# Centring the value rows in the transposing product, and a new order of the steps behind the mixing

## The chip, the cores and the metric

One core of one Trainium2 chip runs the program. The time is device microseconds of an execution; the figure for a kernel is the median of its runs.

## What is computed

The reference is one transformer block with two mixing branches over 16 meta and 512 data tokens, width 1024. Cut to what matters here:

```python
y = rwkv7_scan(rh, heads(decay), kh, vh, kk, ah)      # per head of 64: S += v k^T ..., y = S r
mu = jnp.mean(y, axis=-1, keepdims=True)
var = jnp.mean(jnp.square(y - mu), axis=-1, keepdims=True)
y = ((y - mu) * lax.rsqrt(var + GN_EPS)).reshape(B, T, RW_WIDTH)
y = y * ln_gain.astype(f32) + ln_bias.astype(f32)
bonus = jnp.sum(rh * kh * r_k, axis=-1, keepdims=True) * vh
y = (y + bonus.reshape(B, T, RW_WIDTH)) * g.astype(f32)
...
merged = (sigmoid(gate_sb) * (o_sb @ w_branch_sb) + sigmoid(gate_rw) * (o_rw @ w_branch_rw))
```

The state S is zero at the start, and each value row of it, so each y, is linear in the value vector v of its head: if the mean over a head's 64 values is taken off v, y has the mean zero. The bonus uses v with its mean.

## The kernel before

All activations stand transposed, channels on partitions and tokens along the row, four tiles of 128 channels ("pairs" p of two heads). Each matrix product is made of three: weights and activations are split into a high and a low part (w_hi, w_lo; h_hi, h_lo), and high x high, high x low, low x high are summed in PSUM (`products`, L531 to L541). Weights come in units of 128 x 1024: SyncE fetches a unit into one of four raw buffers, ScalarE writes its high part (`hi_unit`, L525), VectorE its low part (`lo_unit`, L530), into one of two pairs of buffers, which TensorE must have left.

The stages are: norm of the input; 26 units that make the projections; the mixing, in which nine chunks of 64 tokens of the recurrent branch run beside eight heads of attention and ten units of gates, in orders written out by hand for each engine (`ORDER_PE` and so on); the stage behind the mixing, which this change is about; eight branch units; the output product; the FFN.

In a chunk of the mixing, `T0`, `T1`, `T2` (L1488 to L1495) transpose b, k and v of the chunk: products of a 64 x 64 piece with an identity (`st_id`, columns K_IST of the constants tile), two heads apart in the two halves of the partitions. VectorE copies T2's result to v_tm, from where the state and the output take it. `bonus` is made earlier, from vv itself.

Behind the mixing, the order is the list `LATE`, from which each engine takes its own part in the order of the list. Its items are, for r = 0 and 1 (two pairs of heads each, q = 0 and 1): `mean` (TensorE multiplies y with the block matrix `blk`, L1592; VectorE subtracts, L1178; ScalarE squares, L882), `var` (TensorE, L1598; ScalarE square root, L888; VectorE reciprocal, L1182), `gate` (TensorE's gate product, L1604; VectorE y times reciprocal, L1187; ScalarE gain and bias, L894; GpSimd adds the bonus, L692), `out` (VectorE times the gate, L1194; ScalarE high part orw_hi, L899; GpSimd low part orw_lo, L695). `osb` is the split of the attention output (ScalarE osb_hi L876, GpSimd osb_lo L685). Between them stand units: 0 to 5 are gate units (24 products each; ScalarE applies the sigmoid, L915, then splits the weights of the unit two further on), unit 0's products having been made at the end of the mixing already; from 6 on they are branch units. Branch unit 6 multiplies the attention output first (12 products), then waits for all `post` steps of VectorE and GpSimd before the 12 with orw_hi and orw_lo. In the list each engine runs strictly in order:

```python
LATE = [("osb", 0), ("mean", 0), ("unit", 0), ("unit", 1), ("var", 0), ("mean", 1), ("unit", 2), ("gate", 0),
        ("out", 0), ("unit", 3), ("var", 1), ("unit", 4), ("gate", 1), ("out", 1), ("unit", 5)]
```

Of the kernel before, what the change touches and what calls it, by code (L numbers as in the profile page):

```python
# [41 lines left out]
HD = 64  # L42
# [23 lines left out]

K_ID, K_TRI, K_CTRI, K_BLK, K_LT, K_LE, K_IST, K_RST = 0, 128, 256, 384, 512, 576, 640, 704
NK = K_RST + T
# [10 lines left out]
for _p in range(PAIRS):  # L79
# [33 lines left out]

POST_ITEMS = {"mean": (["mean0", "mean1"], ["sq0", "sq1"], ["centre0", "centre1"], []),
              "var": (["var0", "var1"], ["root0", "root1"], ["recip0", "recip1"], []),
              "gate": (["gate0", "gate1"], ["gain0", "gain1"], ["norm0", "norm1"], ["bonus0", "bonus1"]),
              "out": ([], ["hi0", "hi1"], ["out0", "out1"], ["lo0", "lo1"])}

LATE = [("osb", 0), ("mean", 0), ("unit", 0), ("unit", 1), ("var", 0), ("mean", 1), ("unit", 2), ("gate", 0),
        ("out", 0), ("unit", 3), ("var", 1), ("unit", 4), ("gate", 1), ("out", 1), ("unit", 5)]  # L120
LATE += [("unit", i) for i in range(2 * AHEAD, len(MERGE) - EARLY)]
# [120 lines left out]
def build(nc, x, meta, w_in, w_sb, w_rw, w_out, w_g, w_u, w_d, decay_up, aaa_up, gate_up,  # L242
          vecs, g_mix_pre, g_mix_post, g_ffn_pre, g_ffn_post, kf, kb, out):
    with ExitStack() as ctx:
# [463 lines left out]
        def _(act):  # L708
# [161 lines left out]
            for kind, i in LATE:  # L870
                if kind == "osb":
# [4 lines left out]
                    s_.activation(osb_hi[:], qT[:], ACT.Copy).then_inc(osb_h, 1)  # L876
                if kind == "mean":
                    for q in range(2):
                        act.wait_ge(post_dve, upto(POST_DVE, "post", i, f"centre{q}"))
                        if i:  # L880
                            act.wait_ge(post_pe, upto(POST_PE, "post", i - 1, f"var{q}"))
                        s_.activation(ysq[q][:], y_of(2 * i + q), ACT.Square).then_inc(post_act, 1)  # L882
# [109 lines left out]
        def _(dve):  # L992
# [179 lines left out]

            for kind, i in LATE:
                if kind == "mean":
                    for q in range(2):
                        dve.wait_ge(post_pe, upto(POST_PE, "post", i, f"mean{q}"))
                        y = y_of(2 * i + q)
                        v_.scalar_tensor_tensor(y, bank(4 + q), -1.0 / HD, y, ALU.mult, ALU.add).then_inc(post_dve, 1)  # L1178
                if kind == "var":
# [126 lines left out]
        def _(pe):  # L1306
# [111 lines left out]
            def identity(k, p):  # L1418
                return st_id[k, :]

            def of_batch(t, e):
                return lambda k, p: t[k, p // 2, 2 * e + p % 2, :]
# [12 lines left out]
            for kind, n, s in ORDER_PE:  # L1435
# [44 lines left out]
                if kind == "seq":  # L1480
# [9 lines left out]
                    if s in ("T0", "T1", "T2"):  # L1490
                        pe.wait_ge(mix_dve, last_of(MIX_DVE, "seq", c, ("aak", "ark", "arb")))
                        if c != LAST_C:
                            pe.wait_ge(mix_pool, last_of(MIX_POOL, "seq", c, ("bh", "kh")))
                        t = (bt, kt, vv)[int(s[1])]
                        mm = heads(SB_, 128 * int(s[1]), C, 1, [(0, lambda k, p: t[k, p, cols(c)], identity)])  # L1495
                    if s == "Z1":
# [87 lines left out]
            for kind, i in LATE:  # L1584
                if kind == "osb":
                    pe.wait_ge(mix_act, len(MIX_ACT))
                    pe.wait_ge(mix_dve, len(MIX_DVE))
                if kind == "mean":
                    for q in range(2):
                        if i:  # L1590
                            pe.wait_ge(post_dve, upto(POST_DVE, "post", i - 1, f"centre{q}"))
                        t_.matmul(bank(4 + q), blk, y_of(2 * i + q), start=True, stop=True).then_inc(post_pe, 1)  # L1592
                if kind == "var":
# [5 lines left out]
                if kind == "gate":  # L1599
                    for q in range(2):  # L1600
                        if i:
                            pe.wait_ge(post_dve, upto(POST_DVE, "post", i, f"centre{q}"))
                        f0 = (2 * i + q) * P
# [96 lines left out]
def tables():  # L1700
# [11 lines left out]
    f[:, K_LE:K_LE + C] = s <= t  # L1712
    f[:, K_IST:K_IST + C] = s == t
    f[:, K_RST:K_RST + T] = (np.arange(T)[None, :] + PAD) % C != 0
    b = np.zeros((P, NB), np.float32)
# [31 lines left out]
```

## Time and profile before

| | |
|---|---|
| median of 3 runs | 971.79 us (969.87 to 972.54) |
| the profiled execution | 973.85 us |
| its span | 972.1 us, mean granted clock 0.976 |
| TensorE products / weight loads busy | 930.8 us (96%) / 744.4 us |
| VectorE / ScalarE / GpSimd busy | 477.8 / 401.4 / 74.0 us |
| the mixing | from 199 to 450.4 us of the span |
| behind it, to the branch products | 450.4 to 497.6 us |
| from there to the end | 474.5 us |

### The profile page before, as it was taken

To read this page: it belongs to the slowest core of one execution; us is meant where nothing else is said; L and a number is where in the kernel's file an instruction comes from. 1 tells how busy PE (TensorE), PEld (TensorE's weight loads), DVE (VectorE), ACT (ScalarE), POOL (GpSimd) and SP (SyncE) were. 2 spreads that over 40 slices of the span, in tenths; PEclk is the share of its full clock that TensorE was granted. 3 is DMA by queue.
4 is the path that set the end of the run, shared out by engine and by line. 5 is a ranking of instruction groups with operands and counts; after the bars stand their busy time and mean duration, and the time that the engine had idled before them with its cause. 6 is when DMAs were issued, how large, how long until landed. Compare 5 with 4: busy or idle time off the path is not lost.

```text
span 972.1 us, 18946 instructions
## 1 busy us (share of the span) xinstructions
PE 930.8 (96%) x8213; PEld 744.4 (77%) x8213; DVE 477.8 (49%) x618; ACT 401.4 (41%) x576; POOL 74.0 (8%) x99
## 2 busy tenths in 40 slices
PE   4999999989999999999989996999999999999997
PEld 3999999856667777766768785888888888888886
DVE  6357776236575356362657653444444444422243
ACT  5344455356665445454534452332223223221141
POOL 1011212111111011001220000000000000000000
PEclk9999999969899999999989997999999999999999
DMA  8322222301110101121216641223333233332321
GB/s 258 104 85 69 87 65 67 91 19 35 34 35 16 43 17 54 49 60 51 66 38 212 218 138 44 86 86 91 103 97 97 86 96 98 91 104 87 109 87 65
DMA packets 108863, 81.13 MB, mean 83 GB/s; under 512 B 2879, under 2 KB 99433, under 8 KB 108793
## 3 DMA queue, kind: packets, MB, share of 16 engines
q1 hardware_dynamic: 108792, 80.09, 27.2%
q8 instruction: 57, 0.93, 0.4%
q14 instruction: 14, 0.11, 0.0%
HBM read 75.36 MB, written 4.72 MB: 82 GB/s over the span
## 4 chain that ended last, share of the span: by engine, by line
PE 90%; DVE 4%; ACT 3%; issue 1%; POOL 1%; DMA 1%; SPq 0%; POOLq 0%; DVEq 0%; ACTq 0%
PE psum L540 47%; PE psum L1633 16%; PE psum L1395 9%; PE psum L1429 6%; PE psum L1543 3%; PE psum L1565 2%; PE psum L1580 2%; PE psum L1561 2%; DVE y_rec L1182 1%; PE psum L1316 1%; PE psum L1578 1%; ACT w_hi L525 1%; DMA x_in<-in_x 1%; PE psum L1365 0%; PE psum L1349 0%
## 5 line engine op out<-in xcount | busy, mean ns | idle before, releaser
L540 PE MATMUL psum<-h_hi,w_hi 128*128 128x512 f32 (+1 forms) x784 | 247.1, 352 | 3.3 <-DVE h_lo L999 1.7
L540 PE MATMUL psum<-h_lo,w_hi 128*128 128x512 f32 (+1 forms) x784 | 244.0, 348 | 0.0
L540 PE MATMUL psum<-h_hi,w_lo 128*128 128x512 f32 (+1 forms) x784 | 242.9, 346 | 0.0
L540 PEld LDWEIGHTS psum<-h_hi,w_hi 128*128 128x128 f32 x784 | 137.6, 190 | 25.7 <-issue 3.9
L540 PEld LDWEIGHTS psum<-h_lo,w_hi 128*128 128x128 f32 x784 | 136.8, 190 | 19.8 <-issue 1.2
L540 PEld LDWEIGHTS psum<-h_hi,w_lo 128*128 128x128 f32 x784 | 136.9, 190 | 18.7
L530 DVE TENSOR_TENSOR w_lo<-w_raw,w_hi 128x1024 fp32r<-128x1024 f32 x69 | 84.7, 1228 | 120.5 <-ACT w_hi L525 120.1
L1271 DVE TENSOR_TENSOR w_lo<-w_raw,w_hi 128x1024 fp32r<-128x1024 f32 x44 | 53.9, 1225 | 138.7 <-ACT w_hi L977 138.7
L525 ACT ACTIVATE w_hi<-w_raw 128x1024 fp32r<-128x1024 f32 x70 | 73.7, 1054 | 82.1 <-PE psum L1633 63.2
L977 ACT ACTIVATE w_hi<-w_raw 128x1024 fp32r<-128x1024 f32 x44 | 46.5, 1056 | 72.5 <-PE psum L540 72.5
L1633 PE MATMUL psum<-w_hi,act_hi 128*128 128x512 f32 x144 | 45.7, 389 | 0.0
L1633 PE MATMUL psum<-w_hi,act_lo 128*128 128x512 f32 x144 | 45.7, 389 | 0.0
L1633 PE MATMUL psum<-w_lo,act_hi 128*128 128x512 f32 x144 | 45.6, 389 | 0.0
L1543 PE MATMUL psum<-qT,kT 64*128 64x512 f32 (+4 forms) x80 | 35.4, 561 | 3.3 <-DVE tri_r L1092 3.2
L974 ACT ACT_TABLE_LOAD x11 | 14.1, 1283 | 54.8 <-PE psum L540 54.8
L1429 PE MATMUL psum<-h_hi,w_hi 128*128 128x512 f32 x80 | 34.8, 435 | 0.1
L974 ACT ACTIVATE ffn_t<-psum 128x512 f32<-128x512 f32 x22 | 13.2, 600 | 50.5 <-PE psum L540 50.4
L1170 DVE TENSOR_TENSOR scores<-scores,psum 128x128 f32<-128x128 f32 (+4 forms) x40 | 20.9, 523 | 26.5 <-PE psum L1565 26.3
L1113 DVE COPY_PREDICATED x_inv<-byte_masks,psum 128x512 f32<-128x512 uint8 (+1 forms) x25 | 16.9, 677 | 33.8 <-PE psum L1395 33.7
L1429 PE MATMUL psum<-h_lo,w_hi 128*128 128x512 f32 x80 | 32.3, 404 | 0.0
L1429 PE MATMUL psum<-h_hi,w_lo 128*128 128x512 f32 x80 | 32.1, 401 | 0.0
L1633 PEld LDWEIGHTS psum<-w_hi,act_hi 128*128 128x128 f32 x144 | 26.9, 188 | 5.8 <-DVE w_lo L530 0.2
(260 smaller groups left out, 1472.9 us busy)
## 6 DMA issues: line engine op xcount, KB each, us to landing
w_raw<-in_w_in SPq DMA_DIRECT2D x42, 512.0 KB, 3.8
w_raw<-in_w_g SPq DMA_DIRECT2D x22, 512.0 KB, 3.7
w_raw<-in_w_u SPq DMA_DIRECT2D x22, 512.0 KB, 3.7
w_raw<-in_w_d SPq DMA_DIRECT2D x22, 512.0 KB, 3.5
w_raw<-in_w_out SPq DMA_DIRECT2D x8, 512.0 KB, 5.4
kept_gates<-gate_raw SPq DMA_DIRECT2D x10, 256.0 KB, 2.3
sig_t<-kept_gates SPq DMA_DIRECT2D x10, 256.0 KB, 2.9
x_in<-in_x SPq DMA_DIRECT2D x4, 512.0 KB, 6.4
```

Source lines behind the costliest of these rows:

```text
L525: nc.scalar.activation(split(u)[0][:], raw[u % RAW][:], ACT.Copy).then_inc(w_hi_done, 1)
L530: nc.vector.tensor_sub(lo[:], raw[u % RAW][:], hi[:].bitcast(F32)).then_inc(w_split, 1)
L540: mm = nc.tensor.matmul(o, w[:, (w0 + i) * P:(w0 + i + 1) * P], xs[:, k, c0:c1], start=(n == 0), stop=(n == total - 1))
L974: s_.activation(ffn_t[t][:], bank(2 * t), ACT.Sigmoid).then_inc(f_sig, 1)
L977: s_.activation(w_hi[v % SPL][:], raw[v % RAW][:], ACT.Copy).then_inc(w_hi_done, 1)
L1170: v_.tensor_tensor(d, d, psum[0:rows, CBANK, SEQ - WIDTH[j]:SEQ], ALU.subtract).then_inc(mix_dve, 1)
L1271: v_.tensor_sub(w_lo[v % SPL][:], raw[v % RAW][:], w_hi[v % SPL][:].bitcast(F32)).then_inc(w_split, 1)
L1395: mm = t_.matmul(psum[rows(p, hd, moved), bnk + p // 2, o0:o0 + n], w(k, p), m(k, p), start=first, stop=last, skip_group_check=True)
L1429: mm = t_.matmul(bank(GBANK), w[:, k * P:(k + 1) * P], xs[:, k, META:T], start=(k == 0 and i == 0), stop=(k == KT - 1 and i == 2))
L1543: t_.matmul(psum[0:kn, QBANKS[j % 2], 0:WIDTH[j]], kT[lanes, hp, k0:k0 + kn], qT[lanes, hp, SEQ - WIDTH[j]:SEQ], start=True, stop=True).th ...
L1561: t_.matmul(psum[:, CBANK, SEQ - WIDTH[i]:SEQ], tri_r[:, P:2 * P], part[:, OFF[i]:OFF[i] + WIDTH[i]], start=False, stop=False, skip_group_ ...
L1633: mm = t_.matmul(bank(2 * b + h), xs[:, k, P * b:P * b + P], w[:, 512 * h:512 * h + 512], start=(k == 0 and i == 0), stop=(k == n - 1 and ...
```

## The change

It adds a matrix to the constants tile (identity minus 1/64, 64 columns, K_CEN) and uses it as T2's right operand in place of the identity. The four mean products and the four subtractions behind the mixing are left out, together with the waits on them, and the item `mean` becomes `square`. And `LATE` has another order: both `var` items stand earlier, against the units and against `out`.

```diff
--- before.py
+++ after.py
@@ -64,7 +64,7 @@
 NVEC = 42
 
 
-K_ID, K_TRI, K_CTRI, K_BLK, K_LT, K_LE, K_IST, K_RST = 0, 128, 256, 384, 512, 576, 640, 704
+K_ID, K_TRI, K_CTRI, K_BLK, K_LT, K_LE, K_IST, K_CEN, K_RST = 0, 128, 256, 384, 512, 576, 640, 704, 768
 NK = K_RST + T
 
 NB = LEVELS * C
@@ -111,13 +111,13 @@
 BATCHES = [tuple(range(c, min(c + 2, NC_))) for c in range(0, NC_, 2)]
 
 
-POST_ITEMS = {"mean": (["mean0", "mean1"], ["sq0", "sq1"], ["centre0", "centre1"], []),
+POST_ITEMS = {"square": ([], ["sq0", "sq1"], [], []),
               "var": (["var0", "var1"], ["root0", "root1"], ["recip0", "recip1"], []),
               "gate": (["gate0", "gate1"], ["gain0", "gain1"], ["norm0", "norm1"], ["bonus0", "bonus1"]),
               "out": ([], ["hi0", "hi1"], ["out0", "out1"], ["lo0", "lo1"])}
 
-LATE = [("osb", 0), ("mean", 0), ("unit", 0), ("unit", 1), ("var", 0), ("mean", 1), ("unit", 2), ("gate", 0),
-        ("out", 0), ("unit", 3), ("var", 1), ("unit", 4), ("gate", 1), ("out", 1), ("unit", 5)]
+LATE = [("osb", 0), ("square", 0), ("unit", 0), ("var", 0), ("square", 1), ("unit", 1), ("gate", 0), ("unit", 2),
+        ("var", 1), ("out", 0), ("unit", 3), ("gate", 1), ("unit", 4), ("out", 1), ("unit", 5)]
 LATE += [("unit", i) for i in range(2 * AHEAD, len(MERGE) - EARLY)]
 POST_PE, POST_ACT, POST_DVE, POST_POOL = (
     [("post", r, step) for item, r in LATE if item in POST_ITEMS for step in POST_ITEMS[item][e]] for e in range(4))
@@ -874,9 +874,8 @@
                     act.wait_ge(mix_pe, len(MIX_PE))
                     act.wait_ge(eps_ok, 2)
                     s_.activation(osb_hi[:], qT[:], ACT.Copy).then_inc(osb_h, 1)
-                if kind == "mean":
+                if kind == "square":
                     for q in range(2):
-                        act.wait_ge(post_dve, upto(POST_DVE, "post", i, f"centre{q}"))
                         if i:
                             act.wait_ge(post_pe, upto(POST_PE, "post", i - 1, f"var{q}"))
                         s_.activation(ysq[q][:], y_of(2 * i + q), ACT.Square).then_inc(post_act, 1)
@@ -1171,11 +1170,6 @@
                                          ALU.subtract).then_inc(mix_dve, 1)
 
             for kind, i in LATE:
-                if kind == "mean":
-                    for q in range(2):
-                        dve.wait_ge(post_pe, upto(POST_PE, "post", i, f"mean{q}"))
-                        y = y_of(2 * i + q)
-                        v_.scalar_tensor_tensor(y, bank(4 + q), -1.0 / HD, y, ALU.mult, ALU.add).then_inc(post_dve, 1)
                 if kind == "var":
                     for q in range(2):
                         dve.wait_ge(post_act, upto(POST_ACT, "post", i, f"root{q}"))
@@ -1417,6 +1411,9 @@
 
             def identity(k, p):
                 return st_id[k, :]
+
+            def centring(k, p):
+                return consts[k, K_CEN:K_CEN + C]
 
             def of_batch(t, e):
                 return lambda k, p: t[k, p // 2, 2 * e + p % 2, :]
@@ -1492,7 +1489,8 @@
                         if c != LAST_C:
                             pe.wait_ge(mix_pool, last_of(MIX_POOL, "seq", c, ("bh", "kh")))
                         t = (bt, kt, vv)[int(s[1])]
-                        mm = heads(SB_, 128 * int(s[1]), C, 1, [(0, lambda k, p: t[k, p, cols(c)], identity)])
+                        mm = heads(SB_, 128 * int(s[1]), C, 1,
+                                   [(0, lambda k, p: t[k, p, cols(c)], centring if s == "T2" else identity)])
                     if s == "Z1":
                         pe.wait_ge(mix_dve, upto(MIX_DVE, "seq", c, "v"))
                         mm = opening(SB_, 0, C, 0, (0, a_c, whole(s_st)))
@@ -1585,11 +1583,6 @@
                 if kind == "osb":
                     pe.wait_ge(mix_act, len(MIX_ACT))
                     pe.wait_ge(mix_dve, len(MIX_DVE))
-                if kind == "mean":
-                    for q in range(2):
-                        if i:
-                            pe.wait_ge(post_dve, upto(POST_DVE, "post", i - 1, f"centre{q}"))
-                        t_.matmul(bank(4 + q), blk, y_of(2 * i + q), start=True, stop=True).then_inc(post_pe, 1)
                 if kind == "var":
                     for q in range(2):
                         pe.wait_ge(post_act, upto(POST_ACT, "post", i, f"sq{q}"))
@@ -1598,8 +1591,6 @@
                         t_.matmul(bank(6 + q), blk, ysq[q][:], start=True, stop=True).then_inc(post_pe, 1)
                 if kind == "gate":
                     for q in range(2):
-                        if i:
-                            pe.wait_ge(post_dve, upto(POST_DVE, "post", i, f"centre{q}"))
                         f0 = (2 * i + q) * P
                         t_.matmul(bank(2 + 2 * i + q), gup[:, f0:f0 + P], sg[:, META:T], start=True, stop=True).then_inc(post_pe, 1)
                 if kind == "unit":
@@ -1711,6 +1702,7 @@
     f[:, K_LT:K_LT + C] = s < t
     f[:, K_LE:K_LE + C] = s <= t
     f[:, K_IST:K_IST + C] = s == t
+    f[:, K_CEN:K_CEN + C] = (s == t) - 1.0 / HD
     f[:, K_RST:K_RST + T] = (np.arange(T)[None, :] + PAD) % C != 0
     b = np.zeros((P, NB), np.float32)
     for j in range(LEVELS):
```

What stands on TensorE behind the last chunk, before (a_r holds y, consts is blk; of the 24 products of a unit only the first is shown, unit 1 first):

```order
L1592 MATMUL psum<-a_r,consts 128x512 [waits mix_dve,mix_act]
L1592 MATMUL psum<-a_r,consts 128x512
L540 MATMUL psum<-h_hi,w_hi_55 128x512 [waits w_split]
...
L1598 MATMUL psum<-y_sq_157,consts 128x512 [waits post_act]
L1598 MATMUL psum<-y_sq_158,consts 128x512 [waits post_act]
L1592 MATMUL psum<-a_r,consts 128x512 [waits post_dve] x2
L540 MATMUL psum<-h_hi,w_hi_53 128x512 [waits gate_out,w_split]
...
L1604 MATMUL psum<-sig_xg,gate_up_w 128x512 x2
L540 MATMUL psum<-h_hi,w_hi_55 128x512 [waits gate_out,w_split]
...
L1598 MATMUL psum<-y_sq_157,consts 128x512 [waits post_act]
L1598 MATMUL psum<-y_sq_158,consts 128x512 [waits post_act]
```

and in the changed kernel (L1591 is the variance product, L1595 the gate's):

```order
L1591 MATMUL psum<-y_sq_157,consts 128x512 [waits post_act,mix_dve,mix_act]
L1591 MATMUL psum<-y_sq_158,consts 128x512 [waits post_act]
L540 MATMUL psum<-h_hi,w_hi_55 128x512 [waits w_split]
...
L1595 MATMUL psum<-sig_xg,gate_up_w 128x512 x2
L540 MATMUL psum<-h_hi,w_hi_53 128x512 [waits gate_out,w_split]
...
L1591 MATMUL psum<-y_sq_157,consts 128x512 [waits post_act]
L1591 MATMUL psum<-y_sq_158,consts 128x512 [waits post_act]
L540 MATMUL psum<-h_hi,w_hi_55 128x512 [waits gate_out,w_split]
```

The variance product of the first two pairs now stands directly behind the mixing and waits for the squares; the second one stands behind unit 2 where it stood behind unit 3.

ScalarE before: from unit 1's sigmoid (sig_t_146) to the first root (y_rs), and from pair 0's high parts to the second pair's roots (L525 is the high part of a unit's weights):

```order
L915 ACTIVATE sig_t_146<-psum 128x512 [waits w_used]
L525 ACTIVATE w_hi_55<-w_raw_52 128x1024 [waits w_used,w_landed3]
L888 ACT_TABLE_LOAD
L888 ACTIVATE y_rs_161<-psum,small 128x512 [waits post_pe]
...
L899 ACTIVATE orw_hi<-y_o_163 128x512 [waits post_dve]
L899 ACTIVATE orw_hi<-y_o_164 128x512 [waits post_dve]
L915 ACTIVATE sig_t_148<-psum 128x512 [waits w_used]
L525 ACTIVATE w_hi_55<-w_raw_50 128x1024 [waits w_used,w_landed1]
L888 ACT_TABLE_LOAD [waits post_dve]
L888 ACTIVATE y_rs_161<-psum,small 128x512 [waits post_pe]
L888 ACTIVATE y_rs_162<-psum,small 128x512 [waits post_dve,post_pe]
```

and in the changed kernel:

```order
L887 ACT_TABLE_LOAD
L887 ACTIVATE y_rs_161<-psum,small 128x512 [waits post_pe]
L887 ACTIVATE y_rs_162<-psum,small 128x512 [waits post_pe]
...
L914 ACT_TABLE_LOAD
L914 ACTIVATE sig_t_146<-psum 128x512 [waits w_used]
...
L887 ACT_TABLE_LOAD [waits post_dve]
L887 ACTIVATE y_rs_161<-psum,small 128x512 [waits post_pe]
L887 ACTIVATE y_rs_162<-psum,small 128x512 [waits post_dve,post_pe]
L898 ACTIVATE orw_hi<-y_o_163 128x512 [waits post_dve]
L898 ACTIVATE orw_hi<-y_o_164 128x512 [waits post_dve]
L914 ACT_TABLE_LOAD
L914 ACTIVATE sig_t_148<-psum 128x512 [waits w_used]
```

The first roots stand ahead of unit 1's sigmoid and weights, the second ones ahead of pair 0's high parts and of unit 3's sigmoid.

VectorE before, from the first reciprocal to the low part of unit 6's weights:

```order
L1182 RECIPROCAL y_rec_159<-y_rs_161 128x512 [waits post_act]
L1182 RECIPROCAL y_rec_160<-y_rs_162 128x512 [waits post_act]
L1178 SCALAR_TENSOR_TENSOR a_r<-psum,a_r 128x512 [waits post_pe] x2
L530 TENSOR_TENSOR w_lo_54<-w_raw_49,w_hi_53 128x1024 [waits w_hi_done]
L1187 TENSOR_TENSOR a_r<-a_r,y_rec_159 128x512 [waits post_dve]
L1187 TENSOR_TENSOR a_r<-a_r,y_rec_160 128x512 [waits post_dve]
L1194 TENSOR_TENSOR y_o_163<-psum,a_r 128x512 [waits post_pe,post_pool]
L1194 TENSOR_TENSOR y_o_164<-psum,a_r 128x512 [waits post_pe,post_pool]
L530 TENSOR_TENSOR w_lo_56<-w_raw_50,w_hi_55 128x1024 [waits w_hi_done]
L1182 RECIPROCAL y_rec_159<-y_rs_161 128x512 [waits post_act]
L1182 RECIPROCAL y_rec_160<-y_rs_162 128x512 [waits post_act]
L530 TENSOR_TENSOR w_lo_54<-w_raw_51,w_hi_53 128x1024 [waits w_hi_done]
```

and in the changed kernel, from the low part of unit 2's weights to that of unit 5's:

```order
L530 TENSOR_TENSOR w_lo_54<-w_raw_51,w_hi_53 128x1024 [waits w_hi_done]
L1176 RECIPROCAL y_rec_159<-y_rs_161 128x512 [waits post_act]
L1176 RECIPROCAL y_rec_160<-y_rs_162 128x512 [waits post_act]
L530 TENSOR_TENSOR w_lo_56<-w_raw_52,w_hi_55 128x1024 [waits w_hi_done]
L1181 TENSOR_TENSOR a_r<-a_r,y_rec_159 128x512 [waits post_dve]
L1181 TENSOR_TENSOR a_r<-a_r,y_rec_160 128x512 [waits post_dve]
L530 TENSOR_TENSOR w_lo_54<-w_raw_49,w_hi_53 128x1024 [waits w_hi_done]
L1176 RECIPROCAL y_rec_159<-y_rs_161 128x512 [waits post_act]
L1176 RECIPROCAL y_rec_160<-y_rs_162 128x512 [waits post_act]
L1188 TENSOR_TENSOR y_o_163<-psum,a_r 128x512 [waits post_pe,post_pool]
L1188 TENSOR_TENSOR y_o_164<-psum,a_r 128x512 [waits post_pe,post_pool]
L530 TENSOR_TENSOR w_lo_56<-w_raw_50,w_hi_55 128x1024 [waits w_hi_done]
```

The second pair of reciprocals now stands ahead of pair 0's outputs (y_o) and of the low part of unit 5's weights.

## Rows read from the trace of the kernel before

**Rows 1.** The page's part 4: shares of the chain that ended last
```profile
PE 90%; DVE 4%; ACT 3%; issue 1%; POOL 1%; DMA 1%; SPq 0%; POOLq 0%; DVEq 0%; ACTq 0%
```

**Rows 2.** Chain of waits, 436 to 500: start us, us, what
```profile
461.56 6.56 DVE y_rec L1182 x2
...
482.99 6.56 DVE y_rec L1182 x2
```

**Rows 3.** Timeline of PE, 450 to 502: start, duration, line, names, shapes, count [idle before]
```profile
450.40 1.99 PE L1592 MATMUL psum<-a_r,consts 128*128 128x512 f32 x4 [0.48 <-ACT a_r L832]
...
457.79 1.88 PE L1598 MATMUL psum<-y_sq,consts 128*128 128x512 f32 x4
...
461.45 0.39 PE L540 MATMUL psum<-h_lo,w_hi 128*128 128x512 f32 x1
...
466.77 1.88 PE L1604 MATMUL psum<-sig_xg,gate_up_w 128*128 128x512 f32 x4
...
490.69 0.50 PE L540 MATMUL psum<-osb_hi,w_hi 128*128 128x512 f32 x1 [1.86 <-DVE w_lo L530]
...
497.56 0.47 PE L540 MATMUL psum<-orw_hi,w_hi 128*128 128x512 f32 x1 [2.27 <-POOL orw_lo L695]
...
501.94 0.42 PE L540 MATMUL psum<-osb_hi,w_hi 128*128 128x512 f32 x1
```

**Rows 4.** Timeline of ACT, same columns
```profile
450.38 1.91 ACT L876 ACTIVATE osb_hi<-qT 128x2048 fp32r<-128x2048 f32 x1
452.29 0.64 ACT L882 ACTIVATE y_sq<-a_r 128x512 f32<-128x512 f32 x1
...
453.80 1.28 ACT L915 ACT_TABLE_LOAD   x1
455.10 0.60 ACT L915 ACTIVATE sig_t<-psum 128x512 f32<-128x512 f32 x1
455.59 1.05 ACT L525 ACTIVATE w_hi<-w_raw 128x1024 fp32r<-128x1024 f32 x1
...
459.55 1.28 ACT L888 ACT_TABLE_LOAD   x1
460.84 1.27 ACT L888 ACTIVATE y_rs<-psum,small 128x512 f32<-128x512 f32 x2
...
471.74 1.05 ACT L525 ACTIVATE w_hi<-w_raw 128x1024 fp32r<-128x1024 f32 x1
474.69 1.52 ACT L894 ACTIVATE a_r<-a_r,vec_cols 128x512 f32<-128x512 f32 x2 [1.89 <-DVE a_r L1187]
...
478.89 0.64 ACT L899 ACTIVATE orw_hi<-y_o 128x512 fp32r<-128x512 f32 x1 [0.62 <-DVE y_o L1194]
```

**Rows 5.** Timeline of DVE, same columns
```profile
472.82 1.23 DVE L530 TENSOR_TENSOR w_lo<-w_raw,w_hi 128x1024 fp32r<-128x1024 f32 x1 [3.56 <-ACT w_hi L525]
473.97 1.29 DVE L1187 TENSOR_TENSOR a_r<-a_r,y_rec 128x512 f32<-128x512 f32 x2
...
478.16 0.69 DVE L1194 TENSOR_TENSOR y_o<-psum,a_r 128x512 f32<-128x512 f32 x1 [0.57 <-POOL a_r L692]
...
489.47 1.16 DVE L530 TENSOR_TENSOR w_lo<-w_raw,w_hi 128x1024 fp32r<-128x1024 f32 x1
...
493.47 0.69 DVE L1194 TENSOR_TENSOR y_o<-psum,a_r 128x512 f32<-128x512 f32 x1 [1.64 <-POOL a_r L692]
```

**Rows 6.** Stretches: their us, then busy PE PEld DVE ACT POOL, PEclk, DMA, GB/s
```profile
198.30:215.30 17.00, 16.64 (x149) 9.19 (x150) 4.73 (x9) 9.57 (x13) 1.76 (x6) 0.50 0.01 2
259.60:266.20 6.60, 6.60 (x76) 4.59 (x75) 1.59 (x4) 2.31 (x4) 1.63 (x3) 0.50 0.01 2
447.00:450.40 3.40, 1.87 (x66) 1.41 (x64) 0.00 (x0) 1.17 (x4) 0.00 (x0) 1.00 0.02 5
...
498.60:502.00 3.40, 3.40 (x10) 2.63 (x9) 0.15 (x1) 0.00 (x0) 0.00 (x0) 0.50 0.00 0
```

**Rows 7.** The value rows' tile: T2's products, ns min/median/max
```profile
L1395 PE MATMUL psum<-consts,v_t x144: 218/218/267, 230.0 to 442.4; 64*64 64x64 f32 x144
```

## The prediction

> **What bounds the kernel now.** I read the shares of the chain first: TensorE carries nine tenths of the path [rows 1]. So the change can only matter where the chain leaves TensorE. The chain cut to the stretch behind the mixing shows such a place: it runs through the two reciprocals of the first pair and the two of the second, 6.56 us each time [rows 2]. TensorE's own timeline [rows 3] says the same: its work is gapless until 488.8, then it sits idle 1.86 us (for the low part of unit 6's weights) and 2.27 us (for the last low part of the value branch's input, from GpSimd). From the table of stretches [rows 6]: 3.4 us behind the second gap the granted clock is 0.50 (1.2 GHz) where it stood at 1.00 (2.4 GHz) before; the first gap is followed by a stretch of the same length. Twelve products that take 12 x 0.2315 = 2.78 us at the full clock (unit 2's lines: 461.45 to 466.77 for 23) took 497.56 to 501.94, 4.38 us: one such stretch costs 1.6 us. So the stretch is bound by ScalarE and VectorE, which hand work to each other in a fixed order, and TensorE has only some 4 us of slack in it.
>
> **What the change does, part by part.** All clocks below are us from the span's start, on the scale of the profile before.
>
> *Centring in T2.* The chain of nine chunks keeps its instructions; only the right operand of 9 x 16 short products differs. The identity product takes 218 ns [rows 7], and I know of no row where the values of an operand move a duration. Zero, with a bound of some tenths either way. The constants' load grows by 64 of 1104 columns; TensorE doesn't wait for it on the chain. Every buffer behind the constants moves by 256 bytes per partition; zero as well.
>
> *Means removed.* Four products go. A pair costs 1.72 us (466.77 to the unit's next product [rows 3]), so TensorE loses 3.4 us of work. Four subtractions, each no longer than the 0.7 us of a comparable 128x512 step, leave VectorE. None of it is on the chain as such: the first pair hid the wait for the squares.
>
> *Head of the stage.* The first product behind the mixing is now the variance, and it needs the square, which stands behind the 1.91 us copy of osb_hi on ScalarE [rows 4]. It starts when the first square ends, 452.29 + 0.64 + 0.05 = 452.98, where the mean started at 450.40: TensorE sits idle 2.6 us more, 3.0 in all. The nearest rows, idle 1.86 and 2.27, brought the clock down for 3.4 us; I take the same here, 1.6 us. The ends kept for the range: nothing, and 3.3 us, half of the 6.6 us stretch of [rows 6]. Behind it: variance 1.83 us (as the first mean pair), unit 1 5.55 us, so unit 1 ends at 461.96 (before: 457.79).
>
> *First pair's root.* Before, ScalarE took unit 1's sigmoid and weights ahead of it. Now, by the start-to-start steps of [rows 4]: second square ends and table load 453.54, +1.30 sigmoid of unit 0, +0.49 high part of unit 2's weights, +1.07 table load, +1.29 root, which starts at 457.69 where it started at 460.84. Reciprocals +0.72: 458.41, the next VectorE instruction +6.48 (482.99 to 489.47 [rows 5]): 464.89. That is 3.15 us ahead. Unit 1's sigmoid now waits for TensorE (461.96), its weights' high part 462.6; its low part finds VectorE free at 464.89, so the late unit 1 costs nothing there. Norm of pair 0 +1.15, gain +0.72 = 466.76 (472.82, 473.97, 474.69 in [rows 4, 5]); its bonus on GpSimd follows and is done long before it is read.
>
> *Second pair's root, now ahead of pair 0's outputs.* TensorE: unit 1 461.96, gate 1.72, unit 2 5.55: 469.23. **Here the chain runs through TensorE**, since ScalarE takes unit 2's sigmoid (469.28) and weights (469.77) ahead of the table load (470.84), root (472.13), reciprocals (472.85). Before they began at 482.99: 10 us ahead. Most of it is given back: queued behind the reciprocals on VectorE are now pair 0's outputs (479.33; the second before at 478.16), behind which ScalarE waits with the high parts (+0.73 by 478.16 to 478.89 [rows 4, 5]: 480.06, 480.68), a table load (481.31), unit 3's sigmoid (482.61), and unit 5's weights (483.10), which had gone ahead of the second pair's root before.
>
> *Who waits for that.* Unit 5 on TensorE needs the low part, which starts 1.08 behind the high one (471.74 to 472.82): 484.18 + 1.23 + 0.06 (490.63 to 490.69 [rows 3, 5]) = 485.47. TensorE's units 3 and 4 and two pairs end at 469.23 + 2 x 1.72 + 2 x 5.55 = 483.77, so a gap of 1.7 us opens. That is close to the 1.86 us that brought the clock down, so I charge another 1.6 us; zero is its other end. Unit 5 ends at 485.47 + 5.55 + 1.6 = 492.62, branch 0's first half at 495.40.
>
> *The other path into the value branch.* Norm of pair 1 behind unit 5's low part 485.33, gain 486.05, unit 4's sigmoid 487.57, unit 6's high part 488.06, low 489.14, output 490.29, and from an output to the branch's first product 4.09 us (493.47 to 497.56 [rows 3, 5]): 494.38. This is 1.0 us before TensorE arrives, so TensorE ends last here, the gap of 2.27 us is gone, and the slow stretch behind it with it.
>
> *Sum.* Branch 0 ends at 495.40 + 2.78 = 498.18 instead of 501.94: **3.8 us less**. All from there on is released by TensorE's branch products, one every 0.2315 us, and moves with them. Loads are not in the way: the fetch of unit 6's weights is released by unit 2's low part, which ends near 457.6, 30 us before their use, and SyncE's order of fetches is as before. The same five table loads stand in both programs. The profiled execution took 973.85 us (span 972.1), 2.1 over the median; I take the 3.8 off the median of 971.79: 968.0.
>
> A rule that speaks on the two gaps: the Trainium skill's page "TensorE: Matmul & The Clock Gate", section "Why this matters for your kernels", ties a loss of clock to idle gaps longer than either of the two that I expect. The trace before doesn't agree: the clock fell behind gaps of 1.86 and 2.27 us. By the page neither gap would cost anything, which is rival A.
>
> **Rivals.**
> - *A, the clock stays up.* Unit 2 ends at 467.63, all that hangs on it 1.6 earlier; unit 5 483.87 to 489.42, first half 492.20, the output path 492.78, branch end 495.56: 6.4 less, 965.4. For it: the clock stayed at 1.00 in 447.0:450.4 though TensorE was busy only 1.87 of 3.4 us there. Against it: two of two gaps of its size [rows 3, 6]. If just the second gap is spared, the output path ends last (494.38), 4.8 less, 967.0; I count that with the forecast.
> - *B, the first slow stretch is longer*, 6.6 us as at 259.6: unit 2 and all behind it 1.7 us later, 2.1 less, 969.7, which can't be told from no change. For it: the short products of the mixing stand directly ahead, as at 259.6 [rows 6]. Against: behind both gaps ahead of 128-row products it was 3.4 us.
> - *C, slower.* The same place, but 17 us as at 198.3, where TensorE also came out of a wait after a stage switch. From 454.2 to 471.2 at half speed costs 8.5 us: unit 2 ends at 476.1, 6.9 later than forecast, and the second root waits behind it on ScalarE, so everything goes along: 498.18 + 6.9 = 505.1, 3.1 us more than before, 974.9. It turns slower once the stretch costs 5.4 us, that is from 10.8 us of 1.2 GHz on. Against: that row's products use 64 rows; full-height products follow here.
> - *D*: the 256-byte shift or the heavier table disturbs the mixing's many short waits by a us or two, either way. The three runs before already lie 2.7 us apart.
>
> **How the numbers follow.** Forecast with the spared second gap 0.55, A 0.10, B 0.22, C 0.07, D 0.06. 0.3%, 2.9 us, is about what a measurement can tell from no change. The forecast is only 0.9 beyond that, so I give it 0.85 of faster, A 0.95, B 0.3, D a third: 0.47 + 0.09 + 0.07 + 0.02 = 0.65 faster; C and a little of D are slower, 0.08; the rest, 0.27, same. The range runs from A's 965.4 to B with a us for the spread of the runs, 970.7; C lies outside.
>
> **What would show it.** In the changed profile: the first variance product 2.6 us later than the mean was, relative to the last chunk's copy; 0.50 clock for some 3.4 us behind it; the first reciprocal 3.15 us and the third 10 us ahead; pair 0's outputs behind the fourth reciprocal; a gap of 1.7 us ahead of unit 5, released by the low part of its weights; no wait for orw_lo ahead of the value branch. Wrong would be: a wait for orw_lo of over 1 us still there, a slow stretch of over 7 us after 453, or a mixing stage whose length differs by over 1 us.

## The result and the profile after

| | before | changed |
|---|---|---|
| median | 971.79 us (5 runs, 969.87 to 973.12) | 965.6 us (5 runs, 964.74 to 970.14) |
| ratio, 95% interval | | 0.995 [0.9927, 0.9974] |
| profiled execution, span | 973.85, 972.1 | 965.5, 963.7 |
| the mixing (199 us to the last copy into a_r) | 251.0 | 246.5 |
| **the stage** (from there to branch unit 7's first product) | **51.97** | **48.07** |
| from there to the end | 470.16 | 470.12 |

The ratio's interval lies below one (its upper end by 0.26%): the kernel is faster, by about half a per cent. The two spans differ by 8.4 us, the medians by 6.2. The table splits the 8.4: the end is the same to 0.04 us, the stage that the change is about gave 3.9, and the mixing, in which only one operand differs, 4.5. The first of the two was forecast; the second wasn't, and is the first question for the experiments.

From the page of the changed kernel, part 1's TensorE and part 4's shares:

```profile
PE 921.8 (96%) x8205; PEld 739.0 (77%) x8205; DVE 475.8 (49%) x614; ACT 400.8 (42%) x576; POOL 73.9 (8%) x99
...
PE 92%; ACT 2%; DVE 2%; issue 2%; DMA 1%; POOL 1%; SPq 0%; POOLq 0%; DVEq 0%; ACTq 0%
```

TensorE is busy 9.0 us less: 3.4 are the four products; the rest goes with the higher mean granted clock (0.983, before 0.976). It now holds 92% of the chain [rows 1]. The chain cut to the stage, start us, us, what (answers to [rows 2]):

```profile
448.50 3.75 PE psum L1591 x4
452.26 5.89 PE psum L540 x24
...
459.87 5.59 PE psum L540 x24
...
468.33 0.70 ACT y_rs L887
...
472.32 3.29 DVE y_rec L1176
...
477.44 1.28 ACT L914
...
480.31 1.22 DVE w_lo L530
...
488.07 1.30 POOL orw_lo L695
...
490.76 9.33 PE psum L540 x40
```

Pair 0 and pair 1 stand for the items of r = 0 and r = 1 here and below. The chain goes where the prediction sent it: variance on TensorE, unit 1, unit 2, then ScalarE's table load and root, the second pair of reciprocals, pair 0's high parts, the table load for unit 3's sigmoid, unit 5's weights. But at the end it takes the low parts on GpSimd, not TensorE. TensorE's timeline (answers to [rows 3]):

```profile
448.50 3.75 PE L1591 MATMUL psum<-y_sq,consts 128*128 128x512 f32 x4 [3.04 <-ACT y_sq L881]
...
457.99 1.88 PE L1595 MATMUL psum<-sig_xg,gate_up_w 128*128 128x512 f32 x4
...
481.59 0.50 PE L540 MATMUL psum<-h_hi,w_hi 128*128 128x512 f32 x1 [1.56 <-DVE w_lo L530]
...
490.76 0.47 PE L540 MATMUL psum<-orw_hi,w_hi 128*128 128x512 f32 x1 [0.59 <-POOL orw_lo L695]
...
493.58 0.39 PE L540 MATMUL psum<-osb_hi,w_hi 128*128 128x512 f32 x1
```

From the last copy (445.51; before 449.97) the variance starts at +2.99 (forecast +3.01), but the pair takes 3.75 us, not 1.83. The gap ahead of unit 5 is 1.56 us (forecast 1.7), and unit 5 runs on without a loss. The value branch still waits, 0.59 us, where it waited 2.27. ScalarE (answers to [rows 4]):

```profile
453.05 1.27 ACT L887 ACTIVATE y_rs<-psum,small 128x512 f32<-128x512 f32 x2
...
468.33 1.27 ACT L887 ACTIVATE y_rs<-psum,small 128x512 f32<-128x512 f32 x2
476.19 1.23 ACT L898 ACTIVATE orw_hi<-y_o 128x512 fp32r<-128x512 f32 x2 [6.59 <-DVE y_o L1188]
```

The first root starts at +7.54 (before +10.87, forecast +7.72), the second at +22.82 (forecast +22.16), and behind it ScalarE idles 6.59 us until pair 0's high parts. VectorE (answers to [rows 5]):

```profile
451.76 1.75 DVE L530 TENSOR_TENSOR w_lo<-w_raw,w_hi 128x1024 fp32r<-128x1024 f32 x1 [13.11 <-ACT w_hi L525]
453.76 6.56 DVE L1176 RECIPROCAL y_rec<-y_rs 128x512 f32<-128x512 f32 x2 [0.25 <-ACT y_rs L887]
...
469.05 6.57 DVE L1176 RECIPROCAL y_rec<-y_rs 128x512 f32<-128x512 f32 x2 [0.77 <-ACT y_rs L887]
475.53 1.22 DVE L1188 TENSOR_TENSOR y_o<-psum,a_r 128x512 f32<-128x512 f32 x2
480.31 1.22 DVE L530 TENSOR_TENSOR w_lo<-w_raw,w_hi 128x1024 fp32r<-128x1024 f32 x1 [3.56 <-ACT w_hi L525]
...
485.16 1.57 DVE L530 TENSOR_TENSOR w_lo<-w_raw,w_hi 128x1024 fp32r<-128x1024 f32 x1 [2.42 <-ACT w_hi L525]
```

Both pairs of reciprocals, then pair 0's outputs, then unit 5's low part, as the order says. Unit 6's low part (485.16) took 1.57 us (1.16 in [rows 5]), beside GpSimd's bonus; unit 2's (451.76) took 1.75 beside the low part of the attention output on GpSimd:

```profile
447.92 4.52 POOL L685 TENSOR_TENSOR osb_lo<-qT,osb_hi 128x2048 fp32r<-128x2048 f32 x1 [36.56 <-ACT osb_hi L876]
```

And the stretches (answers to [rows 6], same columns):

```profile
200.30:213.80 13.50, 13.45 (x143) 7.72 (x144) 4.09 (x6) 9.19 (x13) 1.75 (x6) 0.50 0.01 2
259.60:266.20 6.60, 6.60 (x110) 5.04 (x100) 2.40 (x4) 4.17 (x6) 0.61 (x1) 1.00 0.00 0
446.00:452.80 6.80, 4.30 (x6) 2.17 (x7) 1.04 (x1) 6.75 (x7) 4.52 (x1) 0.50 0.00 0
481.60:493.60 12.00, 11.41 (x49) 9.06 (x50) 5.54 (x6) 5.62 (x8) 5.11 (x4) 1.00 0.15 44
```

The slow stretch at the head is 6.8 us long, but 2.5 of it fall into TensorE's wait. The second one of the mixing (259.6, 6.6 us before) isn't there, and the first is 13.5 us instead of 17.

### The profile page after: what moved, and what is told of

It reads as the page before. It is cut to its first block, busy times and chain, and to the rows that moved or that the text cites. A ratio compares the mean times of both kernels' runs of the same rounds, so it can differ in the third digit from the quotient of the medians.

```text
span 963.7 us, 18924 instructions
## 1 busy us (share of the span) xinstructions
PE 921.8 (96%) x8205; PEld 739.0 (77%) x8205; DVE 475.8 (49%) x614; ACT 400.8 (42%) x576; POOL 73.9 (8%) x99
## 4 chain that ended last, share of the span: by engine, by line
PE 92%; ACT 2%; DVE 2%; issue 2%; DMA 1%; POOL 1%; SPq 0%; POOLq 0%; DVEq 0%; ACTq 0%
PE psum L540 48%; PE psum L1624 17%; PE psum L1389 9%; PE psum L1426 6%; PE psum L1541 3%; PE psum L1578 2%; PE psum L1563 2%; PE psum L1559 1%; PE psum L1576 1%; PE psum L1310 1%; DMA x_in<-in_x 1%; ACT w_hi L525 1%; PE psum L1359 0%; PE psum L1355 0%; PE psum L1343 0%
## 5 line engine op out<-in xcount | busy, mean ns | idle before, releaser
L525 ACT ACTIVATE w_hi<-w_raw 128x1024 fp32r<-128x1024 f32 x70 | 73.7, 1054 | 81.0 <-PE psum L1624 63.4
L1624 PEld LDWEIGHTS psum<-w_lo,act_hi 128*128 128x128 f32 x144 | 27.0, 188 | 5.7
```

The source lines that it names most:

```text
L525: nc.scalar.activation(split(u)[0][:], raw[u % RAW][:], ACT.Copy).then_inc(w_hi_done, 1)
L1624: mm = t_.matmul(bank(2 * b + h), xs[:, k, P * b:P * b + P], w[:, 512 * h:512 * h + 512], start=(k == 0 and i == 0), stop=(k == n - 1 and ...
```

## The experiments

All stage lengths are from the start of the last chunk's copy into a_r to the first product of branch unit 7, in the profiled execution of each kernel. The first four experiments ran on one chip (the kernel before there: median 971.9 us of 23 runs), the last four on another (971.36 of 23), so ratios are safer than medians between the two groups.

**The changed kernel again.** No edit.

> The changed kernel once more, on the chip of the next three. Stage: from the start of the last chunk's copy into a_r to the first product of branch unit 7; it was 51.97 us before and 48.07 us in the changed kernel. Theory 1 (the stage gave 3.9 us; the other 4.5 us of the two profiles, in the mixing, are a matter of where the slow clock stretches fell in those executions): the stage is again within 1 us of 48.1, the mixing (199 us to that copy) differs from its 246.5 us by anything from 0 to 5 us, and the total is 3 to 5 us below the kernel before. Theory 2 (the changed operand or the moved buffers really shorten the mixing): mixing again about 246.5 us and a total 6 to 8 us below.

Median 967.0 us of 12 runs (964.94 to 970.99), ratio 0.9951 [0.9932, 0.9969]. Stage 48.29, mixing 250.5, end 470.2. Its slow stretches:

```profile
197.60:214.90 17.30, 16.53 (x149) 9.08 (x149) 5.03 (x9) 9.57 (x13) 1.76 (x6) 0.51 0.01 2
259.10:266.40 7.30, 7.30 (x79) 5.08 (x79) 1.93 (x4) 2.85 (x5) 1.81 (x3) 0.53 0.01 2
450.40:457.30 6.90, 4.83 (x7) 2.51 (x8) 1.57 (x1) 6.84 (x8) 4.52 (x1) 0.51 0.00 0
```

The stage repeats to 0.2 us, the mixing does not: here it has both slow stretches, as before, and takes 250.5 us where it took 251.0. So the 4.5 us of the first pair of profiles aren't the change's. Theory 2 falls.

**Means out, old order.**

```diff
-LATE = [("osb", 0), ("square", 0), ("unit", 0), ("var", 0), ("square", 1), ("unit", 1), ("gate", 0), ("unit", 2),
-        ("var", 1), ("out", 0), ("unit", 3), ("gate", 1), ("unit", 4), ("out", 1), ("unit", 5)]
+LATE = [("osb", 0), ("square", 0), ("unit", 0), ("unit", 1), ("var", 0), ("square", 1), ("unit", 2), ("gate", 0),
+        ("out", 0), ("unit", 3), ("var", 1), ("unit", 4), ("gate", 1), ("out", 1), ("unit", 5)]
```

> The centring in T2 stays and the means are left out, but the steps stand in the old order (square where the mean stood). Theory 1 (worked out from durations of the rows before): the means alone free the second square from the reciprocals, so unit 4's weights are split 6 us earlier; the stage takes about 45.8 us with a slow stretch ahead of the value branch, 44.2 without, that is less than the changed kernel's 48.1: the new order costs 2 to 4 us. Rival (the new order is what gives the time): the stage takes 50 us or more here.

Median 963.96 (6 runs), ratio 0.9924 [0.9902, 0.9946]; stage 45.49 (45.8 expected). VectorE behind the first root, then TensorE at the head and ahead of the value branch:

```profile
455.32 6.56 DVE L1176 RECIPROCAL y_rec<-y_rs 128x512 f32<-128x512 f32 x2 [0.65 <-ACT y_rs L887]
461.80 1.16 DVE L530 TENSOR_TENSOR w_lo<-w_raw,w_hi 128x1024 fp32r<-128x1024 f32 x1
462.88 1.28 DVE L1181 TENSOR_TENSOR a_r<-a_r,y_rec 128x512 f32<-128x512 f32 x2
```
```profile
445.86 0.50 PE L540 MATMUL psum<-h_hi,w_hi 128*128 128x512 f32 x1 [0.48 <-ACT a_r L832]
...
486.51 0.47 PE L540 MATMUL psum<-orw_hi,w_hi 128*128 128x512 f32 x1 [2.45 <-POOL orw_lo L695]
```

The first reciprocal starts at +9.9, later than in the changed kernel (+8.25), but unit 4's low part and pair 0's norm follow the reciprocals at once; in [rows 5] they stood at 472.82 and 473.97, 5 us behind them, since the second square waited for its centring, and unit 2's sigmoid and unit 4's weights stood behind that square on ScalarE. No wait at the head beyond the handover's 0.48 us. So leaving the means out gives 6.5 us of stage in the old order, and the new order gives 2.6 of them back (3.0 by the medians, 967.0 and 963.96). That is with a slow stretch behind the 2.45 us wait; the value branch itself starts at +41.1, 4.2 us ahead of the changed kernel's +45.25.

**Centring alone, on the kernel before.**

The edit against the kernel before, cut to the product; the matrix and its 64 columns are added as in the change:

```diff
...
-                        mm = heads(SB_, 128 * int(s[1]), C, 1, [(0, lambda k, p: t[k, p, cols(c)], identity)])
+                        mm = heads(SB_, 128 * int(s[1]), C, 1, [(0, lambda k, p: t[k, p, cols(c)], centring if s == "T2" else identity)])
...
```

> Kernel before with the centring matrix in T2 alone; the mean products and subtractions stay, on rows whose mean is already about zero, and so does the old order. Theory 1: stage 52 us, total within 1.5 us of the kernel before, the mixing scatters by some us between executions in both. Theory 2: the mixing is 4 to 5 us shorter in this kernel too, and so the total.

Median 971.25 (12 runs), ratio 0.9995 [0.998, 1.001]; stage 51.90, mixing 248.7. Operand, longer table and moved buffers cost nothing and give nothing. TensorE's two waits, and the stretches:

```profile
488.40 0.50 PE L540 MATMUL psum<-osb_hi,w_hi 128*128 128x512 f32 x1 [1.87 <-DVE w_lo L530]
...
495.27 0.77 PE L540 MATMUL psum<-orw_hi,w_hi 128*128 128x512 f32 x1 [3.84 <-POOL orw_lo L695]
```
```profile
198.20:215.30 17.10, 16.68 (x149) 9.22 (x150) 4.83 (x9) 9.56 (x13) 1.75 (x6) 0.50 0.01 2
259.60:266.20 6.60, 6.60 (x116) 4.98 (x114) 2.36 (x5) 3.63 (x6) 1.55 (x3) 1.00 0.01 2
495.00:498.40 3.40, 3.13 (x8) 2.48 (x8) 1.22 (x1) 0.21 (x1) 0.13 (x1) 0.50 0.00 0
```

Two things are to be seen. The stretch at 259.6 stands at 1.00 here, with the mixing 2.3 us shorter than before: the same kind of scatter, in a kernel that is not faster. And the first wait, 1.87 us, brought no slow stretch, where 1.86 us did before [rows 3]; only behind the second, 3.84 us, the clock is low. T2's own products in the changed kernel, beside [rows 7]:

```profile
L1389 PE MATMUL psum<-consts,v_t x144: 218/218/267, 228.8 to 437.9; 64*64 64x64 f32 x144
```

**Head filled.** The changed kernel, with two mean products of the first two pairs ahead of the variance, unread.

```diff
+                if kind == "square" and i == 0:
+                    for q in range(2):
+                        t_.matmul(bank(4 + q), blk, y_of(q), start=True, stop=True)
```

> The changed kernel with two mean products of the first pairs put back on TensorE at the head of the stage, their result unread, so that TensorE works 1.8 of the 3.0 us for which it waited for the squares. If the idle wait brings the clock down (Theory 1): the granted clock stays at 1.00 behind the head, the variance pair takes 1.7 instead of 3.75 us, unit 1 ends 2 us earlier against the last copy, and everything behind unit 2 follows: stage 46 us. If the low clock there has another cause: it stays low for some 3 us behind the head, stage 48 us. A filler that only costs: 48 to 50 us.

Median 964.77 (6 runs), ratio 0.9933 [0.991, 0.9956]; stage 46.04. TensorE at the head, and its clock behind it:

```profile
448.06 1.99 PE L1588 MATMUL psum<-a_r,consts 128*128 128x512 f32 x4 [0.48 <-ACT a_r L832]
450.53 1.98 PE L1594 MATMUL psum<-y_sq,consts 128*128 128x512 f32 x4 [0.48 <-ACT y_sq L881]
```
```profile
447.90:460.00 12.10, 11.46 (x38) 7.14 (x39) 5.90 (x3) 11.98 (x15) 4.56 (x1) 1.00 0.15 43
```

The wait is cut from 3.04 us to two of 0.48, the clock stays up, the variance pair takes its usual time, and all of the 2.0 us arrive at the stage's end; the median is 2.2 us below the repeat's. More work on TensorE, less time. A wait of 1.73 us ahead of unit 5 brought no slow stretch either.

**Unit 3 ahead of pair 0's outputs.** `("out", 0), ("unit", 3)` swapped in the changed order.

> The changed order with one swap: unit 3 ahead of pair 0's outputs. The reading of the changed kernel's trace: unit 5's weights wait on ScalarE behind the high parts of pair 0, which wait for two reciprocals, and that opens the gap ahead of unit 5. If so the swap lets ScalarE take unit 3's sigmoid with no table load behind the high parts, TensorE's gap ahead of unit 5 shrinks or goes, and the stage takes about 44.8 us with a slow stretch at the head (changed kernel: 48.1). If the gap has another cause the stage stays at 48.

Median 965.29 (10 runs), ratio 0.9932 [0.9907, 0.9957]; stage 44.67, and TensorE has one wait in it, the one at the head:

```profile
451.03 3.37 PE L1591 MATMUL psum<-y_sq,consts 128*128 128x512 f32 x4 [3.04 <-ACT y_sq L881]
```
```profile
450.50:453.90 3.40, 2.87 (x5) 1.35 (x5) 0.00 (x0) 3.37 (x5) 3.40 (x1) 0.50 0.00 0
```

The stage is 3.4 us shorter than the changed kernel's, but not all of that is the swap's: the slow stretch at the head is 3.4 us long here, 6.8 there, behind the same wait, and unit 1 ends at +11.77 where it ended at +12.48 (+12.71 in the repeat). That leaves about 2.7 us for the swap, which takes away the gap ahead of unit 5: the place named in the prediction gave back much of the early second root. The medians don't settle it: the ratios to the kernel before, 0.9932 and the repeat's 0.9951, have intervals that overlap.

**Mixed order.** Only `LATE` again:

```diff
+LATE = [("osb", 0), ("square", 0), ("unit", 0), ("unit", 1), ("var", 0), ("square", 1), ("unit", 2), ("gate", 0),
+        ("var", 1), ("unit", 3), ("out", 0), ("gate", 1), ("unit", 4), ("out", 1), ("unit", 5)]
```

> Unit 1 back at the head as in the old order, gate 0 and the second root ahead of unit 3, pair 0's outputs behind it. Theory 1 (a gapless head and the second reciprocals right behind the first norm): stage 42.6 us, no slow stretch, 3 us less than the old order without means, total about 961. Rival (an early second root delays unit 4's weights and opens a gap there): 45 us or more.

Median 963.73 (6 runs), ratio 0.9905 [0.9871, 0.9939]; stage 44.05, a miss by 1.5 us. The clock was at 0.50 from 448.0 to 451.4 in this execution, although TensorE had waited only 0.48 and 0.50 us in the 4 us before; so unit 1 took 6.45 us (449.68 to 456.13) instead of the 5.69 of the second experiment. And TensorE still waits twice:

```profile
486.46 0.50 PE L540 MATMUL psum<-osb_hi,w_hi 128*128 128x512 f32 x1 [1.03 <-DVE w_lo L530]
...
490.45 0.47 PE L540 MATMUL psum<-orw_hi,w_hi 128*128 128x512 f32 x1 [0.97 <-POOL orw_lo L695]
```

Ahead of both, VectorE and GpSimd, which the new order makes work at the same time, run longer than elsewhere:

```profile
480.49 2.38 DVE L1181 TENSOR_TENSOR a_r<-a_r,y_rec 128x512 f32<-128x512 f32 x2
```
```profile
480.71 3.31 POOL L695 TENSOR_TENSOR orw_lo<-y_o,orw_hi 128x512 fp32r<-128x512 f32 x2 [9.07 <-ACT orw_hi L898]
483.98 3.58 POOL L692 TENSOR_TENSOR a_r<-a_r,bonus 128x512 f32<-128x512 f32 x2
```

Pair 1's two norms took 2.38 us (1.29 in [rows 5]), the two low parts beside them 3.31 (2.53 in the changed kernel), the bonus 3.58 (2.58). How much of the 1.5 us each of the two gives wasn't separated.

**Both roots ahead of both norms.** Four reciprocal buffers, both gates together.

```diff
-        yrec = [sb(f"y_rec{i}", [P, SEQ]) for i in range(2)]
+        yrec = [sb(f"y_rec{i}", [P, SEQ]) for i in range(4)]
...
+LATE = [("osb", 0), ("square", 0), ("unit", 0), ("unit", 1), ("var", 0), ("square", 1), ("unit", 2), ("var", 1),
+        ("unit", 3), ("gate", 0), ("gate", 1), ("out", 0), ("unit", 4), ("out", 1), ("unit", 5)]
...
```

The reciprocals and norms of r = 0 and 1 use buffers of their own.

> As the last, but both roots ahead of both norms, with a buffer of its own for each of the four reciprocals, and both gates together. TensorE's work in the stage is 40.3 us (four pairs, five units, two halves); this order would bring the stage down to it, 40.6 us, and the total to about 959. Rival: the longer wait for pair 0's norm and GpSimd's four low parts and bonuses in a row end last, 43 us.

Median 961.56 (6 runs, 959.28 to 963.93), ratio 0.9888 [0.9853, 0.9924]: the lowest median of all, 10 us below the kernel before (its interval overlaps those of the mixed order and the old order). Stage 41.76, 1.2 more than the 40.6 expected. TensorE waits ahead of the value branch, and GpSimd's work before that:

```profile
486.27 0.47 PE L540 MATMUL psum<-orw_hi,w_hi 128*128 128x512 f32 x1 [0.39 <-POOL orw_lo L695]
```
```profile
474.08 5.68 POOL L692 TENSOR_TENSOR a_r<-a_r,bonus 128x512 f32<-128x512 f32 x4 [19.74 <-ACT a_r L893]
479.71 3.55 POOL L695 TENSOR_TENSOR orw_lo<-y_o,orw_hi 128x512 fp32r<-128x512 f32 x2
```

The wait is 0.39 us, though two low parts took 3.55 us beside VectorE. With 0.16 us ahead of unit 2 and the handover at the head, 0.43, that is 1.0 of the 1.5 us between 41.8 and TensorE's own 40.3; the rest isn't accounted for. The stage is now all but bound by TensorE.

**Products kept.** The old order without means, with the four mean products back on TensorE, unread.

> The old order without means (stage 45.5 us), with the four mean products put back on TensorE unread, and no subtraction. If what the removal gave was mainly TensorE's 3.4 us of work, the stage goes back to 49 to 52 us. If it was the dependency (the second squares no longer wait for a subtraction queued behind the reciprocals), the products cost only what they push back the first root, 1.8 us: 46 to 47.7 us.

Median 966.66 (10 runs), ratio 0.9946 [0.9923, 0.9969]; stage 46.22, 0.7 more than without them. VectorE as in the second experiment:

```profile
458.31 6.57 DVE L1176 RECIPROCAL y_rec<-y_rs 128x512 f32<-128x512 f32 x2 [0.78 <-ACT y_rs L887]
465.30 1.23 DVE L530 TENSOR_TENSOR w_lo<-w_raw,w_hi 128x1024 fp32r<-128x1024 f32 x1 [0.42 <-ACT w_hi L525]
466.44 1.29 DVE L1181 TENSOR_TENSOR a_r<-a_r,y_rec 128x512 f32<-128x512 f32 x2
```

The norm follows 1.6 us behind the reciprocals (464.88 to 466.44), not 5.9 as in the kernel before (468.12 [rows 2] to 473.97 [rows 5]). The 0.7 us needs a correction: the wait ahead of the value branch, 1.79 us here, brought no slow stretch, the 2.45 us without products did, at 1.6 us. The value branch starts at +47.6 in the kernel before, at +43.4 here and at +41.1 without products; the ratios of the last two to the kernel before, 0.9946 and 0.9924, are 2.1 us apart, with intervals that overlap. So at equal clock the products cost 2.3 us, 1.7 of it by delaying unit 1 and the first root (+10.87 here, +9.17 without them), and the subtractions with the waits on them, behind which the second square stood, the other 4.2 of the 6.5.

## Why the prediction was right, and where it was off

- **What bounds the stage**: right. It was a chain over ScalarE and VectorE, and TensorE had slack.
- **Sum**: 3.8 us were forecast for the stage, 3.9 measured, 3.7 on the repeat. The forecast time, 968.0, lies by the repeat's median of 967.0; 965.6 was a median of five with a range of 5.4 us. That the sum came out so close is partly luck, as the next two points show.
- **Head**: gap and start right (3.0 us). "I take the same here, 1.6 us": mis-sized. From the first variance product to unit 1's end it took 9.49 us (9.72 in the repeat) where 1.83 + 5.55 = 7.38 was forecast without the slow clock, so the price was 2.1 to 2.3 us. The clock was low for 6.8 and 6.9 us in the two profiles of the changed kernel, 2.5 and 2.1 of them inside the wait; the variance pair took 3.75 instead of 1.83 us, and unit 1 ended at +12.48, forecast +11.99.
- **Gap ahead of unit 5**: size and releaser right, "so I charge another 1.6 us" wrong. 1.56 us cost no clock in either profile. So TensorE didn't end last: the output path did, as the branch that the prediction counted with the forecast said, but 0.84 us later than its 494.38 - 449.97 = 44.41 (45.25): 0.5 from the head, 0.3 from unit 6's low part beside GpSimd's bonus. That path's end, 45.25 + 2.82 = 48.07, happens to be where TensorE's forecast end was (498.18 - 449.97 = 48.21): a charge of 1.6 us too much stood in for 0.8 us missing elsewhere and for the other path's lead.
- **Rival A** (the clock stays up) named 965.4, next to 965.6, and is refuted all the same: the clock fell at the head, and filling the wait there gave 2.0 us. The Trainium skill's page "TensorE: Matmul & The Clock Gate", section "Why this matters for your kernels", would have neither gap cost anything. The 3.04 us at the head lie too near the length that the section names to decide it; the traces disagree by their shorter waits, of which 1.86, 2.27 and 2.45 us were followed by 1.2 GHz.
- **B** had the length of the slow stretch about right and its price wrong, since part of it fell into the wait; with unit 3 first it was 3.4 us, the forecast length, at the same place. **C** didn't come.
- **D** was given too little, and one of the prediction's own signs of being wrong came: the mixing's length differed by more than 1 us. It varied from 246.4 to 251.0 us between profiled executions, and not with the kernel: 246.5 and 250.5 for the same program. It goes along with the slow time in it, but only roughly: with 13.5 to 14 us at 0.50 it took 246.5, 246.4 and, with the products kept, 247.7; with 17 us 248.7, 248.6, 249.0, 248.3 and, in the mixed order, 250.2; with 17 and 6.7 us 251.0 and 250.5. Why a stretch falls in one execution and not in the next, and what makes the rest of the scatter, stays open.
- **Not seen**: how much the removals alone would give. The prediction called them worth nothing on the chain ("None of it is on the chain as such"). In the old order they were worth 6.5 us: the subtractions with their waits 4.2, the products 2.3, of which 1.7 came from the first pair ahead of unit 1. The new order was judged only against the old one with means, and so its cost of 2.6 us stayed hidden.

## What to carry to other kernels

When an operation is taken out, follow what stood behind its result on in-order engines, not only its own time: here two subtractions of some 0.6 us, queued behind 6.5 us of reciprocals, held back a square, a sigmoid and the next weights, and were worth 4.2 us. Cost each half of a combined change alone: removal and reordering had opposite signs. And an expensive step moved ahead takes along everything queued behind it on its engine; move it only to where nobody waits for the next in line.

## What the runs showed of the hardware

- A gap doesn't tell by its length alone whether the clock falls: 1.86 us of wait was followed by 3.4 us at 1.2 GHz in the kernel before, 1.87 us in the centring-alone kernel wasn't. Of the stage's other waits, 2.27, 2.45 (old order), 3.04 (the changed kernel twice, and the one with unit 3 first) and 3.84 us all were; 1.56 (twice), 1.73 and 1.79 weren't. And in the mixed order the clock fell at 448.0 behind two waits of only 0.48 and 0.50 us.
- The low clock can begin inside the wait: at 446.0, 0.5 us after TensorE fell idle, and so part of it costs nothing. The same 3.04 us wait brought 6.8, 6.9 and 3.4 us of it in three executions.
- Filling the wait at the head with two unread products made the stage 2.0 us shorter, in one profiled execution, and the median 2.2. The wait isn't all that decides: of the profiled executions, the three with the 3.04 us wait at the head had the low clock there, and of the seven without it one had, in the mixed order.
- VectorE and GpSimd can block each other. In the changed kernel unit 2's low part starts at 451.76 and ends at 453.51, 1.07 us behind the end of GpSimd's operation (447.92 + 4.52 = 452.44): about the 1.16 that such a part takes undisturbed, as if it had done its whole work after that. Unit 6's low part ends as far behind the bonus beside it (485.16 + 1.57 = 486.73, 1.08 behind 483.07 + 2.58 = 485.65). In the mixed order two norms took 2.38 instead of 1.28 us, in the last but one experiment two low parts on GpSimd 3.55 instead of 2.53. The Trainium skill's page "SBUF — State Buffer", section "SBUF: two separate sides", says so: a port pair that the two share is locked for a whole instruction by whichever starts first, among them a VectorE operation with two SBUF inputs against a GpSimd one that reads SBUF. These rows agree, and an order that keeps both busy at once should be costed with it.
